# A hybrid SSD and S5 decoder layer: the mixer's stages in another order, its side work in another grain

## The reference

```python
proj = h @ w_in[l]
z, xbc, dt_raw, u, gates = jnp.split(proj, [OFF_XBC, OFF_DT, OFF_U, OFF_GATES], axis=-1)
gate_a, gate_b = jnp.split(gates, 2, axis=-1)
y_a = ssd_mixer(xbc, z, dt_raw, ...)      # conv, SiLU, chunked scan, * silu(z), RMSNorm by group
p_a = y_a @ w_a_proj[l]
y_b = s5_mixer(u, ...)                    # 64 groups, complex diagonal scan over the tokens
glu_a, glu_g = jnp.split(jax.nn.gelu(y_b) @ w_b_glu[l], 2, axis=-1)
p_b = glu_a * jax.nn.sigmoid(glu_g)
merged = jax.nn.sigmoid(gate_a) * p_a + jax.nn.sigmoid(gate_b) * p_b
x = x + g2 * (merged @ w_out[l])
```

## Time and profile before

| | us |
|---|---|
| median of three runs | 2531.85 (2530.79 to 2532.26) |
| the profiled execution | 2532.31 |
| its span | 2530.6 |
| PE busy in the span | 2413.1 (95%) |
| DVE busy | 1732.4 (68%) |
| ACT busy | 1033.3 (41%) |
| DMA, mean share of 16 engines (queue 1) | 64.8% |

### The profile page before, as it was taken

How to read it: one execution, slowest core, us unless ns; L and a number is a source line. 1 busy time by engine, 2 the same in 40 slices (tenths; PEclk the granted TensorE clock), 3 DMA queues, 4 the chain that set the end, 5 groups by cost and what they waited for, 6 DMA issues and landing times. The chain is left out here.

```text
span 2530.6 us, 39778 instructions
## 1 busy us (share of the span) xinstructions
PE 2413.1 (95%) x16260; PEld 2187.3 (86%) x16260; DVE 1732.4 (68%) x2033; ACT 1033.3 (41%) x1109; POOL 227.6 (9%) x257
## 2 busy tenths in 40 slices
PE   6899999999999998899999979989999999999998
PEld 3488799888899998889999979989788899888998
DVE  3376877778778778898777766666867455444544
ACT  3243343333443443444444433433433444434433
POOL 1422213241313000000000000000000000000000
PEclk9899999999999999999999989999999999999999
DMA  9987877779787765455566657567678556555552
GB/s 359 378 264 251 296 262 260 270 270 320 241 286 278 280 233 182 145 176 182 168 216 218 218 175 272 182 216 271 228 254 307 170 189 198 195 183 182 193 176 98
DMA packets 296989, 584.56 MB, mean 231 GB/s; under 512 B 10324, under 2 KB 35412, under 8 KB 295316
## 3 DMA queue, kind: packets, MB, share of 16 engines
q1 hardware_dynamic: 291408, 559.98, 64.8%
q0 software_dynamic: 4144, 22.28, 2.4%
q10 hardware_dynamic: 1300, 0.35, 0.1%
HBM read 569.98 MB, written 12.58 MB: 230 GB/s over the span
## 5 line engine op out<-in xcount | busy, mean ns | idle before, releaser
L905 DVE TENSOR_TENSOR wlo<-raw,whi 128x1024 fp32r<-128x1024 f32 x800 | 986.1, 1274 | 582.9 <-ACT whi L527 571.4
L527 ACT ACTIVATE whi<-raw 128x1024 fp32r<-128x1024 f32 x800 | 803.2, 1052 | 1232.2 <-PE gps L295 1183.4
L295 PE MATMUL gps<-whi,hs 128*128 128x512 f32 (+1 forms) x2816 | 876.3, 388 | 14.1 <-DVE wlo L905 9.5
L295 PE MATMUL gps<-hs,whi 128*128 128x256 f32 x3584 | 662.5, 287 | 36.5 <-DVE hs L1450 14.9
L295 PEld LDWEIGHTS gps<-whi,hs 128*128 128x128 f32 x2816 | 529.6, 189 | 141.2 <-issue 24.3
L295 PEld LDWEIGHTS gps<-hs,whi 128*128 128x128 f32 x3584 | 564.3, 194 | 49.1 <-issue 28.9
L295 PE MATMUL gps<-wlo,hs 128*128 128x512 f32 (+1 forms) x1408 | 543.3, 386 | 0.0
L295 PE MATMUL gps<-hs,wlo 128*128 128x256 f32 x1792 | 509.6, 284 | 0.0
L295 PE MATMUL gps<-ffs,whi 128*128 128x256 f32 x2752 | 498.8, 284 | 5.6 <-DVE wlo L905 5.6
L295 PEld LDWEIGHTS gps<-ffs,whi 128*128 128x128 f32 x2752 | 429.1, 192 | 7.7 <-DVE wlo L905 6.9
L295 PE MATMUL gps<-ffs,wlo 128*128 128x256 f32 x1376 | 389.3, 283 | 0.0
(11 more groups left out here) (258 smaller groups left out, 1213.8 us busy)
## 6 DMA issues: line engine op xcount, KB each, us to landing
raw<-in_w_ffn_in_dram SPq DMA_DIRECT2D x160, 1024.0 KB
raw<-in_w_ada_dram SPq DMA_DIRECT2D x112, 1024.0 KB
raw<-in_w_in_dram SPq DMA_DIRECT2D x80, 1024.0 KB
raw<-in_w_ffn_out_dram SPq DMA_DIRECT2D x56, 1024.0 KB
pre<-in_w_ada_dram SPq DMA_DIRECT2D x32, 1024.0 KB, 14.5
raw<-in_w_ffn_out_dram SPq DMA_DIRECT2D x40, 768.0 KB
raw<-in_w_a_proj_dram SPq DMA_DIRECT2D x16, 1024.0 KB
raw<-in_w_b_glu_dram SPq DMA_DIRECT2D x32, 512.0 KB
```

Source lines behind the costliest of these rows:

```text
L295: return pe.matmul(out, lhsT, rhs, start=start, stop=stop, skip_group_check=True)
L527: act.activation(whi[:, mpos % SPLIT, h, :], raw[:, pos % RING, h, :], ACT.Copy).then_inc(hi_ready, 1)
L905: ins = dve.tensor_tensor(wlo[:, mpos % SPLIT, h, :], raw[:, pos % RING, h, :], whi[:, mpos % SPLIT, h, :].bitcast(F32), ALU.subtract)
```

## The change

- `plan()` has the order xbc, z, gate_b, b_glu, gate_a, a_proj, w_out.
- The S5's first three blocks take 24 PE steps (6 slabs) in place of 16, and DVE's work on a block is cut at other places: into 2, 3, 3, 4, 4 and 2 instructions for k < 3 (`stops` 2, 5, 8, 12, 16, 18), and into 4, 6, 5 and 3 for the others, where it was 6, 4, 4, 4. With 184 PE steps the S5 ends 6 slabs into gate_b.
- S5, the split of its output and the SSD are one generator (`in_turn`). The SSD starts in gate_b, has 36 PE steps (9 slabs) a group, and runs over b_glu to 4 slabs before gate_a's end; b_glu and gate_a's evacuations lie between its steps.
- There is no wait for the whole y_a. ACT and DVE split it group by group into `ya`, a new place; slab s of a_proj's first group of slabs waits for SSD group s + 1.
- b_glu's evacuation leaves sigmoid(gate_b) * p_b in place of gate_b. The merge is made in a_proj's evacuation, for four tiles at a time: DVE multiplies, adds, ACT rounds to `hs`, DVE writes the low part one slab later. Slab s of w_out's first group waits for merge s + 1 (`merged_lo`).
- Since both the SSD and `ada_end` use bank 3 of `mps`, and their order is now different, PE waits in both directions (`bank3_read`, `bank3_free`).
- `x` is fetched back when four merges are made, and DVE waits for it before w_out's first evacuation, no longer at w_out's start.
- PE's b_glu and a_proj are written out in place of a loop.

```diff
            ("gemm", Phase("xbc", "w_in", OFF_XBC, NT, 3, "conv", "h", False, side="s5")),
            ("gemm", Phase("z", "w_in", 0, NT, 2, "silu", "h", False, side="s5")),
-           ("s5_end", None),
-           ("gemm", Phase("gate_a", "w_in", OFF_GATES, NT, 2, "sig_a", "h", True, side="ssd")),
-           ("gemm", Phase("gate_b", "w_in", OFF_GATES + D, NT, 2, "sig_b", "h", True, side="ssd", last=True)),
-           ("split", None),
-           ("gemm", Phase("a_proj", "w_a_proj", 0, NT, 2, "mul_a", "h", True)),
-           ("gemm", Phase("b_glu", "w_b_glu", 0, U // P, 4, "glu", "yb", False, pair=D)),
+           ("gemm", Phase("gate_b", "w_in", OFF_GATES + D, NT, 2, "sig_b", "h", True, side="ssd")),
+           ("gemm", Phase("b_glu", "w_b_glu", 0, U // P, 4, "glu", "yb", False, pair=D, side="ssd")),
+           ("gemm", Phase("gate_a", "w_in", OFF_GATES, NT, 2, "sig_a", "h", True, side="ssd", last=True)),
+           ("ssd_end", None),
+           ("gemm", Phase("a_proj", "w_a_proj", 0, NT, 2, "mul_a", "ya", True)),
            ("gemm", Phase("w_out", "w_out", 0, NT, 2, "resid", "h", True, gate=1, norm=2)),
...
+        xz = at("xz", R, [P, NT, 2, S])
+        ya = at("ya", R, [P, NT, 2, S], F32R)
+        bc = at("bc", R + 32 * K, [P, 2 * GROUPS, S])
+        ub = at("ub", R + 40 * K, [P, UT, S])
+        ga = at("ga", R + 64 * K, [P, NT, S])
+        gb_most = at("gb_most", 0, [P, NT, S])
+        gb_first = at("gb_first", R + 80 * K, [P, 4, S])
...
-            pool.wait_ge(sem("prod_free"), 1 + (FT + 3) // 4 + D // (COLS // 2))
+            pool.wait_ge(sem("merged"), 4)
...
-                    if ph.evac == "sig_a":
+                    n = 2 * i + g
+                    if ph.evac == "sig_b" and n == 1:
                         act.wait_ge(sem("s5_out"), UT)
-                    if ph.evac == "sig_b":
-                        act.wait_ge(sem("ssd_group_done"), 2 * i + g + 1)
-                    dst, f = {"copy": (ub, ACT.Copy), "silu": (zb, ACT.Silu), "sig_a": (ga, ACT.Sigmoid),
-                              "sig_b": (gb, ACT.Sigmoid)}[ph.evac]
-                    act.activation(dst[:, bass.ds(8 * i + 4 * g, 4), :], out, f).then_inc(psum_free(b), 1)
+                    four = slice(4 * n, 4 * n + 4)
+                    dst, f = {"copy": (ub[:, four, :] if n < 2 else None, ACT.Copy), "silu": (xz[:, four, 1, :], ACT.Silu),
+                              "sig_a": (ga[:, four, :], ACT.Sigmoid), "sig_b": (gb(4 * n, 4), ACT.Sigmoid)}[ph.evac]
+                    act.activation(dst, out, f).then_inc(psum_free(b), 1)
+                elif ph.evac == "mul_a":
+                    n = 2 * i + g
+                    act.wait_ge(sem("merged"), n + 1)
+                    act.activation(hs[:, 4 * n:4 * n + 4, 0, :], ga[:, 4 * n:4 * n + 4, :], ACT.Copy
+                                   ).then_inc(sem("merged_hi"), 1)
                 elif ph.evac == "glu":
                     act.wait_ge(sem("prod_free"), r.p + i * 2 + g + 1)
                     act.activation(sil[:, :, :], out[:, 2:4, :], ACT.Sigmoid).then_inc(sem("silu_ready"), 1)
-                    act.wait_ge(sem("merged"), (ph.q0 + i) * 2 + g + 1)
-                    act.activation(hs[:, bass.ds(4 * (ph.q0 + i) + 2 * g, 2), 0, :], prod[:, :, :], ACT.Copy
-                                   ).then_inc(sem("ff_hi"), 1)
...
+                    act.wait_ge(sem("y_scaled"), i + 1)
+                    act.activation(ya[:, 4 * i:4 * i + 4, 0, :],
+                                   E[1][:, :, :].rearrange("p a b -> p (a b)").rearrange("p (a b) -> p a b", a=4),
+                                   ACT.Copy).then_inc(sem("ya_hi"), 1)
...
-                    for _ in range(4):
+                    for _ in range(6 if k < 3 else 4):
                         yield
                     act.wait_ge(sem("s5_y"), k + 1)
                     act.activation(ub[:, k, :], rs[:, :], ACT.Gelu_apprx_tanh).then_inc(sem("s5_gelu"), 1)
-                    yield
+                    if k + 1 < UT:
...
             def split():
 
-                for b in range(2):
-                    act.wait_ge(psum_free(b), r.q)
-                act.wait_ge(slab_done, r.m)
-                act.wait_ge(sem("ssd_group_done"), GROUPS)
                 act.wait_ge(sem("s5_gelu"), UT)
-                act.activation(hs[:, :, 0, :], xbc[:, 0:NT, :], ACT.Copy).then_inc(sem("y_hi"), 1)
                 act.activation(ybs[:, :, 0, :], ub[:, :, :], ACT.Copy).then_inc(sem("y_hi"), 1)
+                yield
+                yield
 
             def final():
...
-                    owed_taps.append((i, g, 1))
+                    later.append(lambda: taps(i, g, 1))
                 elif ph.evac == "mul_a":
                     dve.wait_ge(slab_done, m_end)
-                    g_t = ga[:, bass.ds(8 * i + 4 * g, 4), :]
+                    n = 2 * i + g
+                    four = slice(4 * n, 4 * n + 4)
+                    g_t = ga[:, four, :]
                     dve.tensor_tensor(g_t, out, g_t, ALU.mult).then_inc(psum_free(b), 1)
+                    dve.wait_ge(psum_free(b), q)
+                    dve.tensor_tensor(g_t, g_t, gb(4 * n, 4), ALU.add).then_inc(sem("merged"), 1)
+
+                    def merged_lo():
+                        dve.wait_ge(sem("merged_hi"), n + 1)
+                        dve.tensor_tensor(hs[:, four, 1, :], g_t, hs[:, four, 0, :].bitcast(F32), ALU.subtract
+                                          ).then_inc(sem("merged_lo"), 1)
+
+                    later.append(merged_lo)
                 elif ph.evac == "glu":
...
                     dve.wait_ge(psum_free(b), q)
-                    dve.tensor_tensor(prod[:, :, :], prod[:, :, :], gb[:, t, :], ALU.mult).then_inc(sem("p_b"), 1)
-                    dve.wait_ge(sem("p_b"), (ph.q0 + i) * 2 + g + 1)
-                    dve.tensor_tensor(prod[:, :, :], prod[:, :, :], ga[:, t, :], ALU.add).then_inc(sem("merged"), 1)
-                    dve.wait_ge(sem("ff_hi"), p + 1)
-                    dve.tensor_tensor(hs[:, t, 1, :], prod[:, :, :], hs[:, t, 0, :].bitcast(F32), ALU.subtract
-                                      ).then_inc(sem("prod_free"), 1)
+                    dve.tensor_tensor(g_t, prod[:, :, :], g_t, ALU.mult).then_inc(sem("prod_free"), 1)
...
+                    stops = (2, 5, 8, 12, 16, 18) if k < 3 else (4, 10, 15, 18)
+                    m = [mag[:, 4 * k + j:4 * k + j + 1].broadcast_to([P, S]) for j in range(4)]
+
+                    def scan(dst, src, j):
+                        return dve.tensor_tensor_scan(dst[:, j, :], m[j], src[:, j, :], 0.0, ALU.mult, ALU.add)
+
                     dve.tensor_tensor(WR, C_, bu[0], ALU.mult)
-                    dve.tensor_tensor(T1, S_, bu[1], ALU.mult)
...
                     dve.tensor_tensor(WR, C_, bu[0], ALU.mult)
+                    dve.tensor_tensor(T1, S_, bu[1], ALU.mult).then_inc(sem("real_products"), 1)
+                    if 2 in stops:
+                        yield
...
                 pe.wait_ge(raw_used, used)
+                if bank3_read:
+                    pe.wait_ge(*bank3_read.pop())
+                if isinstance(c, int):
+                    bank3_sums[0] = c + 1
...
-                if ph.name == "w_out":
-                    pe.wait_ge(sem("prod_free"), r.p + 1)
-                elif ph.name == "a_proj":
+                if ph.name == "b_glu":
                     pe.wait_ge(sem("y_lo"), 1)
-                elif ph.name == "b_glu":
-                    pe.wait_ge(sem("y_lo"), 2)
...
+                            if ph.name == "a_proj" and head and g == 0:
+                                pe.wait_ge(sem("ssd_group_done"), s + 1)
+                            if ph.name == "w_out" and head and g == 0:
+                                pe.wait_ge(sem("merged_lo"), s + 1)
...
+                def bank3_free():
+                    bank3_read.clear()
+                    pe.wait_ge(sem("ada_done"), bank3_sums[0])
...
-                    yield from quarters_of_gates(2 if i else 4)
...
+                    yield from quarters_of_gates(2 if i else 10)
...
+                    yield from quarters_of_gates(4)
...
-                    for _ in range(16):
+                    for _ in range(24 if k < 3 else 16):
...
-                elif kind in ("s5_end", "split"):
-                    for _ in sides["s5" if kind == "s5_end" else "ssd"]:
+                elif kind == "ssd_end":
+                    for _ in sides["ssd"]:
```

More of the change, by code:

```diff
@@ L10 @@
 from contextlib import ExitStack
+from itertools import chain as in_turn
 import concourse.bass as bass
@@ L581, in xbc_silu @@
                 act.wait_ge(psum_free(group % 2), q)
[L582 removed]
+                t = xz[:, 4 * group:4 * group + 4, 0, :] if group < 4 else bc[:, 4 * group - NT:4 * group - NT + 4, :]
                 act.activation(t, t, ACT.Silu).then_inc(sem("xbc_ready"), 1)
@@ L698, in body @@
                         evacuate(ph, i, g, m0 + i * mper + (g + 1) * ph.slabs, r.q + i + 1)
```

(35 more changed lines are left out.)

137 lines of the change are left out of this document (70 added, 67 removed).

## The result

| | before | changed |
|---|---|---|
| median, us | 2531.64 (2530.79 to 2532.26, 4 runs) | 2514.04 (2511.76 to 2516.70, 4 runs) |
| ratio | | 0.9928 (0.9913 to 0.9943) |
| profiled execution, its span | 2532.3, 2530.6 | 2511.8, 2510.0 |

A forecast was written before the change was run, and what follows sets the result against it. PE, busy 95% of the span, bounds the kernel, and only its waits can change. Handovers 25.5 plus S5 5.1, less a_proj 5.2 and SSD 1.5, give 23.9 us off 2531.9: 2508 us, range 2497 to 2522.

The forecast's parts named there:

- Handovers: Waits at a_proj's and w_out's starts and the SSD's last square go: 16.3 + 8.2 + 1.0 = 25.5 us gained.
- S5, the sum: Stages with the S5: PE's waits for `rotated` and `wlo` sum to 20.0 us over the blocks.
- The ledger of DVE: S5: adds up DVE's work per block against its window of PE slabs to give each block's waits.
- S5, the gain: S5 waits fall from 25.1 to 20.0 us, a gain of 5 us, the clock taken as equal on both sides.
- finer cuts hide the S5: Rival: PE waits under 5 us for the S5, 15 to 20 us more off, 2488 to 2493; chance 0.12.
- a_proj: First evacuation of each body: ACT's rounding waits for DVE's sum; new waits of 1.9 and 0.7 us, 5.2 us lost.
- SSD: All four SSD groups and the bank-3 waits: 1.5 us lost, between 0 and 5.
- the further 1.38 us that the prediction named: ACT table change in b_glu: a drain beside the 1.28 us load, from the Trainium skill; estimate up to 4 us longer.
- rival (3): b_glu's evacuation and the SSD get in each other's way, 2 to 6 us a group: 2516 to 2532; chance 0.17.
- rival (5): Slower: ACT's queue in b_glu becomes the pace, 30 us lost if `whi` is 1.9 late per slab, 2538; chance 0.06.
- The sum: Whole kernel: 25.5 + 5.1 - 5.2 - 1.5 = 23.9 us off, giving 2508 us.

The follow-up runs named there:

- wait_all: Changed kernel with a_proj's first matmul waiting for all four SSD groups and w_out's first for all four merges: 2523.13 us, ratio 0.9963.
- old_cuts: Changed kernel with the S5 of before: 4 slabs for every block, DVE's work cut into 6, 4, 4, 4 instructions: 2521.62 us, ratio 0.9956.
- old_cuts_held: As `old_cuts`, with 6 empty slabs between the S5 and the SSD, which stands where the changed kernel has it: 2515.09 us, ratio 0.9931.
- long123: Changed kernel with the 6 slabs in S5 blocks 1, 2 and 3 in place of 0, 1 and 2: 2505.40 us, ratio 0.9895.
- fives: Changed kernel with S5 blocks of 4, 5, 5, 5, 5, 4, 4, 4 slabs, the SSD held back by 2 empty slabs: 2505.42 us, ratio 0.9896.
- the second profile: Profiled execution of the changed kernel run again, nothing edited, in another session; 16.2 us less than before's 2532.3; median of that run 2515.43 us.

## Why the forecast was right, and where it was not

The direction and the range held: 2514.0 in 2497 to 2522. By its steps:

- *Handovers* (25.5 forecast with the SSD's square): right. Both waits are gone, and `wait_all` shows what would have been late in w_out, 7.8 us. Their clock was undercounted, 4.3 us against 2.6: the square's wait of 1.0 us had slow matmuls behind it as well, 1.1 us, and the two handovers' dips were 1.7 and 1.5.
- *S5, the sum*: 20.0 forecast, 18.9 and 20.7 measured. By block it was 1.9 (1.9), 3.8 (2.9), 0.9 (1.1), 4.4 to 5.5 (5.3), 3.1 (2.1) and 4.8 to 5.5 (6.7), forecast in brackets. The ledger of DVE holds to 1 us a block for seven of the eight, and to 2 for the last. Block 1's own sum in it gives 2.8, not 2.9. Of the three `w_ada` slabs among the last block's instructions two stand ahead of `rotated`, as the prediction had it.
- *S5, the gain*: the step "I take the clock behind the longer waits as equal on both sides" failed. It was 3.1 us before and is 5.6 to 7.2. With it the S5's stages gained 0.3 to 3.7 us, not 5. And the 5 us were put down to the grain. With the old grain in the new order the waits are 22.1 and the time is the same: 3.0 of the 25.1 went without any change of grain, 1.4 of them because the last block is no longer drained at z's end (2.5 us before, 1.1 in `old_cuts`), the rest in smaller shifts. That the forecast waits and the measured ones nearly agree in sum was in part luck. The rival "finer cuts hide the S5" is out (18.9 and 20.7 us of waits, not under 5). The rule of the Trainium skill (Perfetto Trace Analysis, Optimizing Scalar/DVE Operations), that breaking up DVE's work may let it complete sooner, did not pay in blocks 0 to 2: cut into six pieces over six slabs they give the time of `old_cuts_held`. In blocks 1 to 3 the same cuts paid (`long123`), where the length of a block changes with its cuts, so no run tells the two apart; none cuts a block of 4 slabs into more than four pieces.
- *a_proj*: place, engine and mechanism right, the terms off. 1.9 forecast and 2.0 measured per wait; the 0.7 behind each did not come, but each wait cost 1.7 us of clock: 7.4 us in place of 5.2. Where the clock did not fall, as behind the first of them in `fives`, a second wait of 0.4 us came.
- *SSD*: 1.5 forecast, 3.3 measured, in 6 waits of under 1 us. Two of 0.9 us have an SSD product on PE start only when DVE's `E` is written. As the timelines read, `E` is late because ACT placed an evacuation's sigmoid, with its table, ahead of `whi`, and DVE's `wlo` stands ahead of `E`; no run tests it. The first is in gate_b:

```profile
1298.80 1.28 ACT L657 ACT_TABLE_LOAD   x1
1300.09 1.03 ACT L657 ACTIVATE gb_most<-gps 128x1024 f32<-128x1024 f32 x1
1301.02 1.99 ACT L537 ACTIVATE whi<-raw 128x1024 fp32r<-128x1024 f32 x2
```

```profile
1302.10 2.36 DVE L914 TENSOR_TENSOR wlo<-raw,whi 128x1024 fp32r<-128x1024 f32 x2 [1.39 <-ACT whi L537]
1304.38 1.22 DVE L1379 TENSOR_TENSOR E<-E,cbm 128x1024 f32<-128x1024 f32 x1
```

```profile
1305.70 1.97 PE L305 MATMUL mps<-xdt,E 128*128 128x64 f32 x16 [0.93 <-issue]
```

  The table takes 1.28 us and the sigmoid starts 1.29 after the table's start, as in the earlier trace rows; the further 1.38 us that the prediction named stand nowhere beside it. The second is at b_glu's end, behind b_glu's own sigmoid and DVE's two products:

```profile
1430.79 1.28 ACT L665 ACT_TABLE_LOAD   x1
1432.08 0.60 ACT L665 ACTIVATE sil<-gps 128x512 f32<-128x512 f32 x1
1437.63 1.97 PE L305 MATMUL mps<-xdt,E 128*128 128x64 f32 x16 [0.88 <-issue]
```

  With one of 0.3 us for an SSD square it makes 1.2 us over b_glu. So the mechanism of rival (3) was there, at far less than its 2 to 6 us a group; rival (5) did not come.
- *The sum*: against the ledger of the second profile, the forecast is 23.9, the measured 16.8. Of the 7.1 between them the clock makes 5.8: 2.6 were counted as a gain behind the handovers, and in all 3.2 more was lost than before (10.6 against 7.4). The SSD adds 1.8 and the S5's waits 0.7; a_proj's waits were 1.2 shorter than forecast. The mis-sized term is the clock: a gain of 2.6 us was counted, a loss of 3.2 was measured. The errors partly cancel, a_proj's waits against the SSD's and the S5's.

## What to carry to other kernels

Where PE is the bound, cost a wait as the wait plus the slow matmuls behind it, and look for these behind every new wait of about 2 us or more: here two waits of 2.0 us cost 7.4, and in other runs the same wait had none. A wait of a queue's head for another engine (ACT's rounding for DVE's sum) belongs behind the next piece of the main stream. And a change of grain moves everything behind it, as `old_cuts` showed with 6 us: before a gain is put down to the grain, hold what follows in its place with empty steps.
